# Two decoder blocks in one launch: the mixer norm's factors spread by DMA instead of by TensorE

## The reference

```python
def hgrn2_mixer(q, f_pre, i, g, lb, norm_g):
    ...
    o = hgrn2_chunk_scan(qh, 1.0 - fgate, split(i), jnp.log(fgate))
    o = rms_norm(o, norm_g) * jax.nn.silu(split(g))
    return o.reshape(B, L, HG_WIDTH).astype(q.dtype)

def mla_mixer(c_q, c_kv, k_pe, q_norm_g, w_q_b, kv_norm_g, w_kv_b, cos, sin):
    q = (rms_norm(c_q, q_norm_g) @ w_q_b).reshape(B, L, MLA_HEADS, QK_NOPE + QK_ROPE)
    q_nope = q[..., :QK_NOPE]
    q_pe = apply_rope(q[..., QK_NOPE:], cos[:, None, :], sin[:, None, :])
    kv = (rms_norm(c_kv, kv_norm_g) @ w_kv_b).reshape(B, L, MLA_HEADS, QK_NOPE + V_HEAD)
    ...
y_a = hgrn2_mixer(...) @ w_hg_o
y_b = mla_mixer(...) @ w_mla_o
gate_a, gate_b = jnp.split(jax.nn.sigmoid(gates + b_gate[l]), 2, axis=-1)
mixed = (gate_a * y_a + gate_b * y_b) @ w_out[l]
```

## Time and profile before

| What | us |
|---|---|
| median of 3 runs | 927.5 |
| lowest and highest of them | 927.08, 928.26 |
| the profiled execution's own time | 927.46 |
| its span in the profile | 925.7 |
| PE busy in the span | 903.5 |
| DVE, ACT, POOL busy in the span | 678.7, 465.2, 222.9 |
| granted TensorE clock over the span | 0.999 of full speed |

### The profile page before, as it was taken

One profiled execution on the slowest core, in us unless ns is written; L12 is line 12 of the kernel. 1 busy time (PEld: TensorE's weight loads), 2 busy tenths in 40 slices (PEclk: granted clock), 3 DMA queues, 4 the chain that ended last, 5 costly groups with the idle time before them and its releaser, 6 DMA issues.

```text
span 925.7 us, 16815 instructions
## 1 busy us (share of the span) xinstructions
PE 903.5 (98%) x6767; PEld 799.8 (86%) x6767; DVE 678.7 (73%) x1274; ACT 465.2 (50%) x936; POOL 222.9 (24%) x120
## 2 busy tenths in 40 slices
PE   8999999999999999999999999999999999999997
PEld 7879999989999888888888799887888888888885
DVE  6924986658655888766676767867888888788885
ACT  6334336564443574434444646776734345544343
POOL 3523421441212211642314342221100211210121
PEclk9999999999999999999999999999999999999999
DMA  8454443234333655655545354224545455455531
GB/s 297 164 188 159 162 142 136 99 113 137 131 122 123 230 178 191 227 183 201 192 160 221 136 190 151 110 90 157 184 153 212 182 182 211 159 222 182 209 110 46
DMA packets 23181, 153.67 MB, mean 166 GB/s; under 512 B 2864, under 2 KB 3248, under 8 KB 5568
## 3 DMA queue, kind: packets, MB, share of 16 engines
q1 hardware_dynamic: 22384, 150.43, 45.9%
q0 software_dynamic: 576, 2.10, 0.6%
q10 hardware_dynamic: 144, 0.07, 0.0%
HBM read 151.28 MB, written 1.05 MB: 165 GB/s over the span
## 4 chain that ended last, share of the span: by engine, by line
PE 61%; DVE 25%; ACT 9%; issue 4%; DMA 0%; DVEq 0%; SPq 0%; ACTq 0%
PE pb L506 59%; DVE wl L515 10%; ACT wh L512 4%; DVE FA L515 4%; DVE FA L521 3%; ACT FA L512 3%; DVE FA L518 3%; PE pb L509 2%; DVE wh L530 1%; ACT R L512 1%; DVE X L521 1%; DVE R L521 1%; DVE st L518 0%; DMA X<-in_x 0%; DVE FA L524 0%
## 5 line engine op out<-in xcount | busy, mean ns | idle before, releaser
L506 PE MATMUL pb<-R,wh 128*128 128x256 f32 (+2 forms) x2224 | 551.5, 327 | 5.9 <-ACT R L512 2.0
L506 PE MATMUL pb<-R,wl 128*128 128x256 f32 (+1 forms) x1512 | 423.9, 282 | 0.0
L506 PEld LDWEIGHTS pb<-R,wh 128*128 128x128 f32 x2224 | 371.9, 189 | 46.4 <-ACT R L512 3.5
L515 POOL TENSOR_TENSOR wl<-raw,wh 128x1024 fp32r<-128x1024 f32 (+1 forms) x80 | 195.0, 2442 | 634.3 <-ACT wh L512 525.1
L515 DVE TENSOR_TENSOR wl<-raw,wh 128x1024 fp32r<-128x1024 f32 (+1 forms) x198 | 263.1, 1350 | 82.4 <-ACT wh L512 80.8
L506 PEld LDWEIGHTS pb<-R,wl 128*128 128x128 f32 x1512 | 286.2, 189 | 2.5 <-issue 0.6
L512 ACT ACTIVATE wh<-raw 128x1024 fp32r<-128x1024 f32 (+1 forms) x219 | 222.7, 1044 | 53.4 <-PE pb L506 51.5
L506 PE MATMUL pb<-wh,R 128*128 128x512 f32 (+2 forms) x724 | 235.0, 389 | 2.3 <-ACT R L512 1.0
L506 PEld LDWEIGHTS pb<-wh,R 128*128 128x128 f32 (+1 forms) x724 | 134.5, 187 | 35.4 <-ACT R L512 2.4
L512 ACT ACTIVATE FA<-pb 128x256 f32<-128x256 f32 (+7 forms) x240 | 94.1, 414 | 127.1 <-PE pb L506 116.0
L506 PE MATMUL pb<-wl,R 128*128 128x512 f32 (+2 forms) x372 | 144.4, 388 | 0.0
(11 more groups left out here) (122 smaller groups left out, 478.5 us busy)
## 6 DMA issues: line engine op xcount, KB each, us to landing
raw<-in_w SPq DMA_DIRECT2D x137, 1024.0 KB, 4.8
X<-in_x SPq DMA_DIRECT2D x2, 512.0 KB, 4.5
raw<-in_w SPq DMA_DIRECT2D x2, 512.0 KB, 6.3
post<-in_ffn_post SPq DMA_DIRECT2D x2, 512.0 KB, 4.5
post<-in_w POOLq DMA_DIRECT2D x2, 512.0 KB, 5.2
FA<-in_w POOLq DMA_DIRECT2D x2, 512.0 KB, 8.6
out<-X SPq DMA_DIRECT2D x4, 256.0 KB, 2.0
cst<-in_cst SPq DMA_DIRECT2D x1, 821.5 KB, 12.0
```

The source lines that it names most:

```text
L506: return self.real.matmul(*a, **k) if self.real else self
L515: return self.real.tensor_tensor(*a, **k) if self.real else self
```

## The change

TensorE's part of `o_scale` is gone. Two steps come in its place, both on ACT's DMA queue. `o_spread` stores `r8` (128 x 256, 128 KB) to a new HBM tensor, `factors`. `o_fetch` waits for that store and loads the eight needed rows back, each into all 128 partitions, with two DMAs of four heads (512 KB each) into `RS`, 2048 columns of `FA`. The multiplication in `o_scale` now reads `RS` in SBUF in place of a PSUM bank, and waits for both loads. `RS` lies where the later gate tiles (`GA1`) go, so the evacuation of a gate tile from 8 on waits for the last multiplication. All four `o_scale` move in the list. Two stand later: 0 goes from behind `kv` 0 to behind `qn` 4, and 2 from behind `kv` 1 to behind `qn` 6. Two stand earlier: 4 goes from behind `qpe` 2 to behind `qpe` 0, and 6 from behind gate 14 to behind `qpe` 1.

```diff
-    segs.append(("latent", p.take(), [[("o_norm",)] + [("o_scale", h) for h in range(0, 8, 2)]] + heads))
+    segs.append(("latent", p.take(), [[("o_norm",), ("o_spread",), ("o_fetch",)] + [("o_scale", h) for h in range(0, 8, 2)]] + heads))
...
-    "latent": "...a.......a..a...........a.b....b.fgf.b..e.f.g.e.dc.f.ba...c.ge.i.cg.ecdh.dh....i...i.h.d.ih",
+    "latent": "...a.....a...a......a..a..a.a..b....b.fgf.b..e.f.g.e.dc.f.b...c.ge.i.cg.ecdh.dh....i...i.h.d.ih",
...
+        RS = fa(10368, 2048).rearrange("p (h t) -> p h t", h=8)
...
-                elif kind == "o_scale":
-                    h0, = a
-                    b = bank(step, B4)
-                    e.wait_ge(*dve.at("o_norm"))
-                    for i in range(2):
-                        r = 32 * ((h0 + i) % 4) + (h0 + i) // 4
-                        m = e.matmul(b[:, 256 * i:256 * i + 256], ident[:, r:r + 1].broadcast_to([128, 128]), r8,
-                                     start=True, stop=True)
-                    m.then_inc(*pe.up(step))
...
                         if n >= 8:
                             e.wait_ge(*pe.at(("read", 1, 1)))
+                            e.wait_ge(*dve.at(("o_mul", 6)))
...
+                elif kind == "o_spread":
+                    e.wait_ge(*dve.at("o_norm"))
+                    e.dma_start(dr["factors"], r8).then_inc(*out_factors.up("all", by=16))
+                elif kind == "o_fetch":
+                    rows = dr["factors"].rearrange("(j x) t -> x j t", x=32)
+                    e.wait_ge(*out_factors.at("all"))
+                    for g in range(2):
+                        e.dma_start(RS[:, 4 * g:4 * g + 4, :], rows[g].partition_broadcast(128)).then_inc(*in_spread.up(g, by=16))
...
                     e.wait_ge(*dve.at(("read", h0 // 4, h0 // 2 % 2)))
-                    e.wait_ge(*pe.at(step))
-                    e.tensor_tensor(ov.rearrange("p h t -> p (h t)"), ov.rearrange("p h t -> p (h t)"), banks.of(step)[:, :],
-                                    ALU.mult).then_inc(*dve.up(("o_mul", h0)))
-                    banks.ended(step, dve.now())
+                    e.wait_ge(*in_spread.at(1))
+                    e.tensor_tensor(ov, ov, RS[:, h0:h0 + 2, :], ALU.mult).then_inc(*dve.up(("o_mul", h0)))
```

More of the change, by code:

```diff
@@ L605, in program @@
         in_w1 = [signal(f"in_w1_{i}") for i in range(2)]
-        in_nk, in_sk = signal("in_nk"), signal("in_sk")
+        in_nk, in_sk, in_spread, out_factors = signal("in_nk"), signal("in_sk"), signal("in_spread"), signal("out_factors")
         out_done = signal("out_done")
-        every = [pe, act, dve, pool, in_xm, in_id, in_gain, in_sm, in_cst, in_lev, out_done] + in_x + in_first + in_slab + in_w1 + [in_nk, in_sk] \
+        every = [pe, act, dve, pool, in_xm, in_id, in_gain, in_sm, in_cst, in_lev, out_done] + in_x + in_first + in_slab + in_w1 + [in_nk, in_sk, in_spread, out_factors] \
             + list(in_post.values())
@@ L2313 @@
         dr[n] = nc.dram_tensor("in_" + n, a.shape, mybir.dt.from_np(a.dtype), kind="ExternalInput").ap()
+    dr["factors"] = nc.dram_tensor("factors", (128, 256), FP, kind="Internal").ap()
     dr["out"] = nc.dram_tensor("out_0", (1, 256, D), FP, kind="ExternalOutput").ap()
```

## The result

| What | before | after |
|---|---|---|
| median, us | 927.6 (4 runs) | 937.96 (4 runs) |
| lowest, highest | 927.08, 928.26 | 937.2, 938.69 |
| the profiled execution's own time | 927.46 | 937.71 |
| its span | 925.7 | 935.9 |
| granted TensorE clock over the span | 0.999 | 0.990 |

The changed kernel is slower, at a ratio of 1.0106 with a 95% interval of 1.0093 to 1.0118: about 10 us. The prediction was 930.1, with 933.0 at the top of its range. Its sign was right and its size was not.

The account below looks back on a forecast made before the run. PE, busy for 98% of the span, was taken to bound the kernel. Gate 10 3.45 us late, less 0.87 for the removed fourth spreading, gave 2.6 us on 927.46: 930.1 us, range 927.7 to 933.0.

Parts of the forecast that it names:

- Removed from PE, 3.5 us: Stage latent: four spreadings by TensorE removed, 0.87 us each, 3.5 us in all, all on the path.
- ACT's queue, 0 us: Store and loads issued on ACT behind the splits of units 50 and 51: delay taken as 0.
- `qn` 3 at 201.0: PE without spreading in the second `kv` starts `qn` 3 at 201.0, 2.1 us ahead of before.
- The load, landing between 5.2 and 8.6 us after its issue: Second load of factors, issued at 197.3, lands at 202.5 to 205.9; first multiplication starts at 204.5.
- The rival of the late load: Load landing past 204.5 moves `o_scale` 0 and all behind it: 931.5, or 933 at 10 us; chance 0.13.
- The stalls, 6.25 us, and +2.6 in all: PE waits at `qpe` 0, 2, 3, gate 8, 9 total 6.25 us; gate 10 3.45 late, less 0.87: 2.6.
- The prediction's own check: Check of the sum: PE saves 3.5 of work and 0.3 at `qn` 3, gains 6.25 us of stalls.
- I see no place that gives it back.: Behind gate 10, DVE and PE stay late by the same 3.45 us, with no PE idle time to recover it.
- The wait at gate 8, two SBUF inputs: Added wait before gate 8's evacuation costs nothing; two-SBUF-input multiplications miss POOL's split, else 1.2 us more, once.
- The rival that the gain stays: PE's banks free in time, so only savings of 3.5 and 0.3 count: 923.6; chance 0.12.

Follow-up runs that it names:

- pe_order: Kernel before, spreading by TensorE and no DMA, with only the four `o_scale` moved to the changed kernel's places; 931.52 us, ratio 1.0041.
- no_load: Changed kernel without the store and the loads, multiplying by whatever lies in `RS`; 931.73 us, ratio 1.0037.
- pe_late: Kernel before, spreading by TensorE, with only the four `o_scale` moved behind gate 8, 10, 12 and 14; 928.5 us, ratio 1.0009.
- late_pin: `late_packed` with `tm2` 0 and `tm1` 0 of the maps stage fixed to PSUM banks 2 and 3; 926.1 us, ratio 0.9977.
- half_wait: Changed kernel with a semaphore per load, so heads 0 to 3 wait for the first load alone; 931.85 us, ratio 1.0037.
- distinct: Changed kernel with loads of 1 KB pieces where each partition reads its own, out of the weights; 931.42 us, ratio 1.0034.
- packed: Changed kernel with factors stored so that each partition reads one 4 KB piece per load; 931.65 us, ratio 1.0034.
- late_packed: Changed kernel with 4 KB pieces, three loads into other space, `o_scale` behind gate 8, 10, 12, 14, no gate 8 wait; 926.1 us, ratio 0.9984.

## Why the prediction was right or wrong

- **Removed from PE, 3.5 us.** No run shows this term alone. Under the changed order it is worth nothing (`pe_order` and `no_load` take the same time), and behind the gate tiles 2.6 us of it show: from their pieces at 189 us to their last ones `pe_late` takes 722.58 and `late_pin` 719.94.
- **ACT's queue, 0 us.** Right in size. The issues took 0.35, 0.38 and 0.53 us and `no_load` gains nothing over `half_wait`. The times were off: the second load was issued at 195.62 and not at 197.3. The loads stand in the list behind a split on ACT, and went out before it ran:

```profile
195.21 0.94 ACTq L545 DMA_DIRECT2D FA<-factors  x2
```

```profile
196.31 1.05 ACT L512 ACTIVATE wh<-raw 128x1024 fp32r<-128x1024 f32 x1
```

This made the load 1.7 us earlier and, by luck, hid part of what follows.
- **`qn` 3 at 201.0.** It began at 201.37, with the common 0.38 of start taken off 200.99.
- **The load, landing between 5.2 and 8.6 us after its issue. This is the step that failed.** The second load took 15.3. The landing was to be bounded by two rows, and had it come by 8.6 us after the true issue, at 204.2, DVE would not have waited. It waited 5.99 us. The two rows that I took as ends are of loads in which each partition reads its own bytes, and `distinct`, which does the same in 1 KB pieces, indeed took 6.3. The row that would have borne on 1 KB pieces read by all did not exist, and the prediction said so in a sentence and then did not widen the bound for it. The rival of the late load had the mechanism right, each microsecond past the need moving all behind it, with too small a size: 933 at most, at 0.13. The figure weighed beside it, the Trainium skill's, DMA: Bandwidth & Descriptors, section Anatomy of one DMA, gives an estimated 3.2 us for 512 KB. The section is on DMAs issued by GpSimd, and these loads were issued by ACT. The loads of 512 KB in the page of before took 4.5 to 8.6 in the median of each kind, GpSimd's own 5.2 and 8.6, and the second load here 15.3.
- **The stalls, 6.25 us, and +2.6 in all.** Right, tile by tile, where the load is in time. From the piece at 189 to that at 911 us `half_wait` stands 3.61 us behind the kernel before, `no_load` 3.59 and `distinct` 3.63. Less the 0.98 of the stage maps this is 2.6 in each. `packed` stands 4.53 behind: the 0.68 of its half clock and 0.29 in the long piece of 944 matmuls come on top. The prediction's own check, 6.25 less 3.5 and 0.3, gives 2.45 and not 2.6, which changes nothing here. In the changed kernel gate 10 came at 227.36 (without the common 0.38) in place of 221.3: 6.0 late, the 5.99 us that DVE waited for the load.
- **"I see no place that gives it back."** None does, but one takes more: 0.98 us in the stage maps, by the rotation of the PSUM banks. The step looked at the banks of the three rings 0 to 2 near the change and not at the ring 4 to 7 from which `o_scale` took a bank.
- **The wait at gate 8, two SBUF inputs.** Both cost nothing, as forecast; the multiplications took 0.69 us in place of 0.68, as POOL was idle then.
- **The rival that the gain stays.** Wrong for this order. The other order shows that 1.5 to 2.1 us of it can be had (`late_packed` and `late_pin`).

The sum of the parts: 2.6 for the order, 6.0 for the load, 1.0 for the banks and 0.2 for scatter, 9.8 of the 10.24 us between the last pieces; the common start of 0.38 is the rest, within rounding. The 2.6 was measured without the load, in `half_wait`, `no_load` and `distinct`, and the 6.0 is DVE's wait.

## What to carry to other kernels

Price a transfer by a row of the same shape, size of piece and sharing of source included, and where there is none, let the range say so or lay the source out in larger pieces. Before work is taken off the busiest engine, look at where the rest of that step will stand in the other engines' lists: here DVE's list ahead of four short tiles decided, and the same step two places further on turned a loss into a gain. A step that takes or drops a PSUM bank also turns the bank order of everything behind it, and the chain of waits of a far stage is where this shows.

## What had not been expected of the hardware

- Loads of 1 KB pieces that all 128 partitions read from the same rows cost 106 ns a packet, those with rows of their own 51 ns; two loads of 512 KB in one queue took 8.6 and 15.3 us, in the median of the two 6.3 with rows of their own and 6.6 as 4 KB pieces. Slabs of 1 MB in the other queue took 14.7 and 10.8 us beside the slow load, and 4.8 before.
- The store in the order that makes these pieces took 1.10 us to issue, where the plain one took 0.35.
- DMA issues on ACT's queue went out ahead of activations that stand before them in the list (the loads at 195.21, the copy and the split ahead of them at 195.81 and 196.31).
- With PE idle for 7.4 us the granted clock fell to 0.50; from 220 to 222 us it read 0.61 and from 222 on 1.00. In `half_wait`, `no_load` and `packed` it also fell at 210 to 212 us, behind idle times of 1.3, 0.3 and 2.0 us, and in `distinct`, with the same idle times, it did not. What tells them apart stays open.
